# Attention scores of two heads at once: plain rows in halves of the array, rotary rows in quarters

## The reference

```python
def mla_dense(qn, qr, kn, kr, v):
    s = jnp.einsum('bqhd,bkhd->bhqk', qn, kn) + jnp.einsum('bqhd,bkd->bhqk', qr, kr)
    p = jax.nn.softmax(s.astype(jnp.float32) * MLA_SCALE, axis=-1).astype(v.dtype)
    return jnp.einsum('bhqk,bkhd->bqhd', p, v)
```

## Time and profile before

| | before |
|---|---|
| median of three runs | 4079.25 us (4078.5 to 4080.53) |
| profiled execution, its own time | 4078.63 us |
| its span | 4076.9 us |
| TensorE busy | 3979.0 us, 98% of the span |
| VectorE busy | 2047.5 us, 50% |
| ScalarE busy | 1070.0 us, 26% |
| L965, scores, TensorE, x800 records | 339.9 us |
| L1036 x2624 and L1026 x1280 | L1036 3% and L1026 2% of the chain that ended last |
| mean granted TensorE clock | 0.992 of full |

### The profile page before, as it was taken

How to read it: one execution, slowest core, us unless ns; L and a number is a source line. 1 busy time by engine, 2 the same in 40 slices (tenths; PEclk the granted TensorE clock), 3 DMA queues, 4 the chain that set the end, 5 groups by cost and what they waited for, 6 DMA issues and landing times.

```text
span 4076.9 us, 77681 instructions
## 1 busy us (share of the span) xinstructions
PE 3979.0 (98%) x31395; PEld 2863.8 (70%) x31396; DVE 2047.5 (50%) x4419; ACT 1070.0 (26%) x2422; POOL 305.1 (7%) x320
## 2 busy tenths in 40 slices
PE   8999999999999899999999999999999999999998
PEld 5565777655544688888888565777544448899997
DVE  1235676666645533333334444666544456444445
ACT  2335555400012111111111334555301121101013
POOL 0000000000000111111111000000000003010101
PEclk9999999999999899999999999999999999999999
DMA  6211000334434488888887221000333348999998
GB/s 212 67 54 62 19 19 19 104 103 118 121 112 156 161 265 273 268 265 266 266 266 229 88 72 62 19 19 19 94 109 88 117 174 255 325 329 326 330 326 281
DMA packets 559541, 658.02 MB, mean 161 GB/s; under 512 B 21284, under 2 KB 496120, under 8 KB 559352
## 3 DMA queue, kind: packets, MB, share of 16 engines
q1 hardware_dynamic: 527768, 564.10, 42.9%
q0 software_dynamic: 31008, 89.20, 7.7%
q10 hardware_dynamic: 576, 2.10, 0.1%
HBM read 582.92 MB, written 72.42 MB: 161 GB/s over the span
## 4 chain that ended last, share of the span: by engine, by line
PE 90%; DVE 4%; DVEq 2%; SPq 1%; DMA 1%; issue 1%; ACT 1%; POOL 0%; POOLq 0%; ACTq 0%
PE PS L750 37%; PE PS L1385 11%; PE PS L1416 9%; PE PS L754 8%; PE PS L965 7%; PE PS L1156 5%; PE PS L1036 3%; PE PS L870 2%; PE PS L1026 2%; DVE arena L1853 2%; SPq L493 1%; PE PS L1410 1%; PE PS L928 1%; DVE arena L2120 1%; DVEq L2124 1%
## 5 line engine op out<-in xcount | busy, mean ns | idle before, releaser
L750 PE MATMUL PS<-arena 128*128 128x160 f32 (+4 forms) x7004 | 1686.9, 402 | 10.9 <-DVE arena L1853 4.9
L750 PEld LDWEIGHTS PS<-arena 128*128 128x128 f32 x7004 | 1102.5, 190 | 567.9 <-issue 543.8
L1853 DVE TENSOR_TENSOR arena<-arena,PS 128x256 f32<-128x256 f32 (+3 forms) x661 | 290.6, 448 | 1035.0 <-ACT arena L1816 556.5
L1853 DVE TENSOR_TENSOR arena<-arena 128x1024 f32<-128x1024 f32 (+9 forms) x778 | 547.6, 721 | 129.2 <-PE PS L750 45.8
L754 PEld LDWEIGHTS PS<-arena 128*128 128x128 f32 (+1 forms) x2980 | 348.1, 142 | 197.4 <-issue 160.1
L754 PE MATMUL PS<-arena 128*128 128x128 f32 (+1 forms) x2980 | 436.7, 278 | 24.2 <-DMA arena<-x_mid,arena 15.4
L1385 PE MATMUL PS<-arena 128*64 128x128 f32 x8192 | 454.9, 273 | 1.6 <-DVE arena L1853 1.6
L1385 PEld LDWEIGHTS PS<-arena 128*64 128x64 f32 x8192 | 451.2, 137 | 5.2 <-DVE arena L1853 1.7
L1416 PE MATMUL PS<-arena 128*64 128x256 f32 x3600 | 396.0, 380 | 1.0 <-DVE arena L1853 0.5
L1816 ACT ACTIVATE arena<-PS 128x160 f32<-128x160 f32 (+1 forms) x256 | 74.5, 291 | 1177.2 <-PE PS L750 636.6
L1416 PEld LDWEIGHTS PS<-arena 128*64 128x64 f32 x3600 | 274.6, 137 | 117.0 <-issue 10.1
(11 more groups left out here) (274 smaller groups left out, 2635.9 us busy)
## 6 DMA issues: line engine op xcount, KB each, us to landing
arena<-in_w_exp_gate SPq DMA_DIRECT2D x128, 1024.0 KB, 7.3
arena<-in_w_exp_up SPq DMA_DIRECT2D x128, 1024.0 KB, 9.6
arena<-in_w_exp_down SPq DMA_DIRECT2D x128, 1024.0 KB, 7.6
arena<-in_w_ada POOLq DMA_DIRECT2D x40, 1024.0 KB, 5.6
arena<-in_w_in SPq DMA_DIRECT2D x32, 512.0 KB, 5.4
h_transposed<-arena SPq DMA_DIRECT2D x20, 512.0 KB, 3.9
q_latent_attn<-arena SPq DMA_DIRECT2D x18, 512.0 KB, 2.8
arena<-q_latent_attn SPq DMA_DIRECT2D x18, 512.0 KB, 3.5
```

The source lines that it names most:

```text
L750: m = pe.matmul(o, lt, rh, start=start and i == 0, stop=stop and i == n - 1)
L1853: return dve.tensor_tensor(o, x, y, op)
```

## The change

The scores of both heads of a unit are made together. Keys lie in two buffers: `kN`, plain rows, head A of a pair on partitions 0 to 63 and B on 64 to 127, and `kR`, the rotary key four times, on each quarter of the partitions. The queries of a tile likewise: four pairs of plain rows, four pairs of rotary rows with each head's twice (`qrx` is copied twice over). Per full unit the score products are: four of 32 rows and 512 keys, one in each quarter of the array (both heads, both key chunks), which start the accumulation; then two of 64 rows and 512 keys (one head in each half) for chunk 0, the same for chunk 1; and for the last 256 keys two of 32 rows and two of 64. A's scores are always in banks 0 to 2, B's in 3 to 5, the band in 0 to 2, the outputs in bank 5, the turned divisors in bank 7, and transposes take banks 6 and 7 in turn.

TensorE's order per unit becomes: long rotary products of the next unit, A's first transposes, plain products 0, A's second, plain products 1, A's third, W's first two, the last 256 keys of the next unit, W's third, B's three, band of the next unit, outputs of the window, outputs of A and B, divisors. ScalarE makes exp A and exp B of the next unit one after the other, with a new wait of each for the transposes that read the same buffer; VectorE copies A0, B0 and B1 (three chunks) and takes the maxima of both heads chunk by chunk. `band` is the former window part of `scores` with its set fixed and its wait changed to `pM` 2N+1. The projection writes keys, queries and rotary queries with one instruction each.

```diff
-qrx = at(R + 21248, MH + 1, 2 * ROPE)
+qrx = at(R + 21248, MH, 2, ROPE)
...
-kT = at(O, MH, TOK)
+kN = at(O, MH // 2, TOK)
+kR = at(O + 5120, TOK)
...
-def score_set(part, n):
-    return (3 * n + PART[part]) % 2 * 3
-def out_bank(n):
-    return score_set("A", n + 1) + 1
-def turned(part, n, ci, blocks):
-    b = 6 + ci % 2 if part == "W" else 7 - ci % 2
-    if part == "B" and ci == 2:
-        b = score_set("A", n + 1) + 2
-    return PS[:, b, 0:blocks * P]
...
-ON_DVE = {"A": (0,), "W": (0, 2), "B": (0,)}
+SET = {"A": 0, "W": 0, "B": 3}
+OUT = 5
+def turned(part, lp, ci, blocks):
+    nth = "AWB".index(part) * (3 if lp is not None else 1) + ci
+    return PS[:, 6 + nth % 2, 0:blocks * P]
+ON_DVE = {"A": (0,), "W": (), "B": (0, 1)}
...
-        def scores(p, lp, n, part):
...
+        def keys(p, lp, n):
...
+            def cols(i):
+                return slice(i * 512, min((i + 1) * 512, TOK if full else CTX))
+            def rotary(g, i, quad):
+                rows, k = slice(quad * ROPE, (quad + 1) * ROPE), cols(i)
+                pe.matmul(PS[:, 3 * g + i, 0:k.stop - k.start], qMt[rows, u, 4 + c, :], kR[rows, k], start=True, stop=False)
+            def plain(i):
+                k = cols(i)
+                for g in range(2):
+                    pe.matmul(PS[:, 3 * g + i, 0:k.stop - k.start], qMt[half(g), u, c, :], kN[half(g), c, k], start=False, stop=True).then_inc(s["sM"], 1)
+            def free():
+                if c == 0:
+                    pe.wait_ge(*s(f"q_in{u}", (p + n // 8) * 32 + 32))
+                if later(N):
+                    pe.wait_ge(*s("mxW", 2 * N))
+                    pe.wait_ge(*s("pM", 2 * N))
+            def short(i):
+                if not full:
                     free()
...
-            def some(i):
-                if i == order[0] and part == "A":
-                    if c == 0:
-                        pe.wait_ge(*s(f"q_in{u}", (p + n // 8) * 32 + 32))
-                    if later(N):
-                        pe.wait_ge(*s("mxW", 2 * N))
-                if i == order[0] and part == "B":
-                    pe.wait_ge(*s("pM", 2 * N + 1))
-                if i == 1 and part == "B" and later(N):
-                    pe.wait_ge(*s("ob", N))
-                cn = min(512, nk - i * 512)
-                pe.matmul(PS[:, b + i, 0:cn], qMt[0:rows, u, at_h, :], kT[0:rows, at_h, i * 512:i * 512 + cn], start=True, stop=True).then_inc(s["sM"], 1)
-            return [lambda i=i: some(i) for i in order]
-        def transposes(p, lp, n, part, ahead=False):
+                elif N > 1:
+                    pe.wait_ge(*s("ob", N - 1))
+                for g in range(2):
+                    rotary(g, i, 2 * g)
+                plain(i)
+            def long_rotary():
...
+                    for i in range(2):
+                        rotary(g, i, 2 * g + i)
+            return [long_rotary, lambda: plain(0), lambda: plain(1), lambda: short(2)] if full else [lambda: short(0)]
...
+                if later(N) and (part, ci) == (("A", 1) if full else ("W", 0)):
+                    pe.wait_ge(*s("rt_o", N))
...
-                elif (part, ci) == ("W", 2):
+                elif part == "W":
+                    pe.wait_ge(*s("pt_a", pa_count(l, lp, n, 1 + ci)))
+                elif part == "B" and ci < 2:
+                    pe.wait_ge(*s("pt_a", pa_count(l, lp, n, 4 + ci)))
+                elif part == "B":
                     pe.wait_ge(*s("pt_d", pd_count(l, lp, n, 2)))
-                elif (part, ci) == ("B", 0):
-                    pe.wait_ge(*s("pt_a", pa_count(l, lp, n, 3)))
-                elif (part, ci) == ("B", 1):
-                    pe.wait_ge(*s("pt_d", pd_count(l, lp, n, 3)))
-                elif (part, ci) == ("B", 2) and ahead:
...
-        def outputs(p, lp, n, ahead):
...
+        def band_outputs(p, lp, n, ahead):
...
-                if ahead:
-                    pe.wait_ge(*s("pM", 2 * N + 3))
+            if ahead:
+                pe.wait_ge(*s("pM", 2 * N + 4))
+            if later(N):
+                pe.wait_ge(*s("ob", N))
...
+            if not full:
                 pe.wait_ge(*s("pt_a", pa_count(l, lp, n, 3)))
             nm = 10 if full else 2
             for kt in range(nm):
-                if kt in (4, 8):
-                    pe.wait_ge(*s("pt_a", pa_count(l, lp, n, 3 + kt // 4)))
+                if kt == 4:
+                    pe.wait_ge(*s("pt_d", pd_count(l, lp, n, 3)))
+                if kt == 8:
+                    pe.wait_ge(*s("pt_a", pa_count(l, lp, n, 6)))
                 for g in range(2):
-                    pe.matmul(PS[half(g), o, P:2 * P], V[:, kt, half(2 * c + g)], PT[:, place("AB"[g], n, kt), :], start=kt == 0, stop=kt == nm - 1)
+                    pe.matmul(PS[half(g), OUT, P:2 * P], V[:, kt, half(2 * c + g)], PT[:, place("AB"[g], n, kt), :], start=kt == 0, stop=kt == nm - 1)
             pe.wait_ge(*s("rc", N + 1))
             for j in range(2):
-                m = tr(PS[:, o, (2 + j) * P:(3 + j) * P], rcb[:, j, :])
+                m = tr(PS[:, 7, j * P:(j + 1) * P], rcb[:, j, :])
             m.then_inc(s["pv"], 1)
...
-            for part in "AW":
-                weave(scores(p, lp, 0, part), [])
-            weave(scores(p, lp, 0, "B"), transposes(p, lp, 0, "A"))
+            weave(keys(p, lp, 0), [])
+            band(p, lp, 0)
         def pair(p, t0, lp, lp_next):
             for n in range(8):
                 nx = after(lp, n, lp_next)
-                keys = scores(p, *nx, "A") if nx else []
-                turns = transposes(p, lp, n, "W")
-                band = scores(p, *nx, "W") if nx else []
-                weave(keys[:2], turns[:1])
-                for step in keys[2:] + turns[1:] + band + transposes(p, lp, n, "B", bool(nx)):
+                ks = keys(p, *nx) if nx else []
+                turns = [step for part in "AWB" for step in transposes(p, lp, n, part)]
+                weave(ks[:3], turns[:3])
+                if lp is not None:
+                    order = turns[3:5] + ks[3:] + turns[5:]
+                else:
+                    order = ks[3:]
+                for step in order:
                     step()
-                outputs(p, lp, n, bool(nx))
                 if nx:
-                    weave(scores(p, *nx, "B"), transposes(p, *nx, "A"))
+                    band(p, *nx)
+                band_outputs(p, lp, n, bool(nx))
+                outputs(p, lp, n)
...
-                m = A(kT[half(g), g::2, ds(t * P, P)], heads(half(g), 5), ACT.Copy)
-            m.then_inc(s["kn"], 1)
+            A(kN[:, :, ds(t * P, P)], pairs(5), ACT.Copy).then_inc(s["kn"], 1)
...
-                    m = A(qMs[half(g), g::2, :], heads(half(g), 4), ACT.Copy, scale=MSCALE)
-                m.then_inc(s["qn"], 1)
+                A(qMs[:, 0:4, :], pairs(4), ACT.Copy, scale=MSCALE).then_inc(s["qn"], 1)
...
-            A(kT[NOPE:MQ, 0::2, ds(t * P, P)], PS[NOPE:MQ, 2, 0:P].unsqueeze(1).to_broadcast([ROPE, 4, P]), ACT.Copy)
-            A(kT[0:NOPE, 1::2, ds(t * P, P)], PS[0:NOPE, 2, 0:P].unsqueeze(1).to_broadcast([NOPE, 4, P]), ACT.Copy).then_inc(s["kT_cp"], 1)
+            A(kR[:, ds(t * P, P)], PS[:, 2, 0:P], ACT.Copy).then_inc(s["kT_cp"], 1)
...
+            if prev:
+                act.wait_ge(*s("tr", tr_count(l, *prev, part, len(chunks(part, *prev)) - 1)))
...
+                copy_chunks(p, lp, n, "A")
                 copy_chunks(p, lp, n, "W")
                 if nx:
-                    expo(p, *nx, "A")
+                    expo(p, *nx, "A", (lp, n))
+                    expo(p, *nx, "B", (lp, n))
                 copy_chunks(p, lp, n, "B")
                 if nx:
                     expo(p, *nx, "W")
                 rows_sum(p, n)
-                if nx:
-                    copy_chunks(p, *nx, "A")
-                    expo(p, *nx, "B")
...
-            rope(qrx[:, 1:, 0:ROPE], PS[:, 3, 0:MH * ROPE].rearrange("p (h c) -> p h c", h=MH), tab[:, 128:192], MH, 8, tmpm)
-            dve.drain()
-            dve.tensor_copy(qrx[:, 0, 0:ROPE], qrx[:, MH, 0:ROPE]).then_inc(s["qro"], 1)
+            rope(qrx[:, :, 0, :], PS[:, 3, 0:MH * ROPE].rearrange("p (h c) -> p h c", h=MH), tab[:, 128:192], MH, 8, tmpm)
+            dve.drain()
+            dve.tensor_copy(qrx[:, :, 1, :], qrx[:, :, 0, :]).then_inc(s["qro"], 1)
...
-            for g in range(2):
-                dve.tensor_scalar(qMs[half(g), 1 - g::2, :], PS[half(g), 3, :].rearrange("p (h c) -> p h c", h=4), MSCALE, None, ALU.mult).then_inc(s["qM_cp"], 1)
+            dve.tensor_scalar(qMs[:, 4:8, :].rearrange("p a b -> p (a b)"), PS[:, 3, :], MSCALE, None, ALU.mult).then_inc(s["qM_cp"], 2)
...
+                if nth == 0:
                     between()
-                dve.wait_ge(*s("sM", sM_count(l, lp, n, part, nth)))
-                dve.tensor_reduce(mxc[:, g, i:i + 1], PS[:, b + i, 0:min(512, TOK - i * 512)], AX.X, ALU.max)
-            dve.drain()
```

(73 more changed lines are left out.)

111 lines of the change are left out of this document (23 added, 88 removed).

## The result

The changed kernel takes 4232.41 us (median; 4230.65 to 4236.47) where the kernel before takes 4079.89 (4078.5 to 4081.17): a ratio of 1.0375, interval 1.0362 to 1.0388, 152.5 us slower. The forecast was 4244, with a range of 4185 to 4305. The profiled execution has a span of 4231.2 us, 154.3 more than before.

The account below looks back on a forecast made before the run. TensorE's own list bounds the kernel. Ordinary units +110, edge units +41, last units -8, context +13, first units +11 make 167; projection -2 gives +165 us, so 4244 us, range 4185 to 4305.

Parts of the forecast that it names:

- What bounds it: Attention's full units: bound by the length of TensorE's own list, which repeats after 12.81 us.
- Four quarters at once, -0.86: Score products per unit: rotary rows run in four array quarters at once, 3.44 us in place of 4.30.
- Rival (b): Rotary score passes: quarters run two at a time (4299 us) or one by one (4437); 14%.
- Eight more changes, +1.45: TensorE's order per unit: 12 changes of array division where there were 4, 5x0.20 + 3x0.15 = 1.45 us.
- Waits, +1.69: TensorE per unit: W1 waits 0.33 us for A2's copy; 1.36 us standing still behind B0's copy and exp B.
- Edge and last units: 16 band-edge units take 14.77 us, +41 us together; each layer's last unit takes 9.4, giving -8 us.
- Context and first units: Context units +0.9 us each, +13 with the turn to full ones; first unit of each layer +4 and +7.
- Projection: Before attention: fewer ScalarE and VectorE operations, VectorE's scaling then ending last; -1.1 us a layer, -2 in all.
- (a): Full units: divisions cost as said but the wait chain is covered, unit 13.40 us, 4141 in all; 5%, half-way cases 7%.
- (c): TensorE's clock falls during the 1.4 us of waits, passes doubling in parts: 64 x 3 us, 4436; 3%.
- (d): Full units: the saving of 0.86x64 = 55 us shows whole, 4024 us; 3%.
- (e): Whole kernel: saving and costs cancel, no difference, 4079 us; 1%.

Follow-up runs that it names:

- The control: Kernel before plus four small 16-column products on all 128 rows in every full unit, woven into transposes: 4123.29 us, against 4077.78.
- the order alone: Changed kernel with its order, banks, copies and waits, but scores from before's keys, queries and full-array products: 4191.15 us, ratio 1.0276.
- the kernel with products on 64 rows: Kernel before plus four small 16-column products on rows 0 to 63 in every full unit, woven into transposes: 4203.35 us, against 4077.78.
- products on 32 rows: Kernel before plus four small 16-column products on rows 0 to 31 in every full unit, woven into transposes: 4202.19 us, against 4077.78.

## Why the prediction was right, point by point

- **What bounds it.** TensorE's own list, 12.81 us a unit. The control bears this out: four small products of 0.17 us each by their starts lengthened the period by 0.71 (13.52).
- **Four quarters at once, -0.86.** Right. A quarter pass of 512 columns takes 1.07 us with its changes, a pass of halves 1.06, so four run as freely as two. Of the Trainium skill's 3.07x for four row tiles (TensorE: Matmul & The Clock Gate, Part 3), which would have added an estimated 0.39 us per unit, nothing is seen here: the two rotary passes side by side take 1.49 for 1.29 of columns, and the missing 0.20 is there with halves too. Rival (b) falls.
- **Eight more changes, +1.45.** Right in sum, within what the trace can tell: 14.88 - 12.81 + 0.86 less the waits of 1.47 leaves 1.46. From quarters to halves took 0.20 (0.63 from 628.72 to 629.35 for 0.43 of columns), where 0 to 0.4 was open. The Trainium skill's rule that a new tiling mode drains TensorE (TensorEngine Tiling (Array Packing), Key Properties) agrees; its price here is 0.15 to 0.2 us.
- **Waits, +1.69.** Right in kind, 0.2 too large. W1's was 0.26 (forecast 0.33). From W2's start to the outputs it is 3.96 us (629.98 to 633.95) where the sum had 4.11 (4.26 less the change ahead of it), so TensorE stands for 1.21 in place of 1.36. The term that was too large is the 0.16 from the end of a copy or an exponential to TensorE. It was read from the lengths of two records (0.70 against 0.60), but by starts it is 0.06: B0's copy ends at 631.94 (631.26 and 0.68) and B2 starts at 632.00, exp B ends at 633.89 and the outputs start at 633.95. The first maximum, on the other hand, starts 0.05 later than the sum has it (630.12, 0.14 behind W2's start, for 0.09), and the reductions take the 1.14 that were said. These 0.07 and 0.15 are the whole of 15.10 less 14.88, and of the 13 us by which the 62 periods fell short.
- **Edge and last units.** 14.56 for 14.77 and 9.08 for 9.4, by the same terms.
- **Context and first units.** A context unit takes 5.6 us (+0.9, as said). The first period is 7.79 instead, and the clock accounts for it: see below. +4.4 to the first copy was forecast at +3; the clock, lower there for longer than before, is the likely reason, and no run separates it.
- **Projection.** TensorE starts at 336.99 instead of 337.96, 0.97 earlier (forecast 1.1), and behind VectorE's scaling, which now ends last, as forecast:

```profile
335.98 0.69 DVE L1992 TENSOR_SCALAR arena<-PS 128x512 f32<-128x512 f32 x1 [3.93 <-PE PS L742]
...
336.99 0.70 PE L904 MATMUL PS<-arena 32*128 32x256 f32 x4 [1.15 <-DVE arena L1992]
```

- **The other rivals.** (a), the chain covered: no, the waits are in every unit. (c), the clock halved inside units: no, 1.00 from 480 to 870 us; only its small form holds, at the start and at the turn to full units (0.83 from 395 to 405 us). (d) and (e): no gain shows, since the order alone loses 113 us before the tiling is made.

The rest of the program, +2.1 us, isn't explained; the same stretch differs by up to 5 us among the kernels here (1156.5 to 1162.0) which are alike in it. Not tried: the outputs in the columns of bank 5 that B's last 256 keys leave free (256 to 511). Exp B doesn't read them, so the outputs might not have to wait for it.

## What to carry over

Price a change of the array's division at 0.15 to 0.2 us each and count the changes before the columns saved: eight of them ate 0.86 us of saved streaming and 0.6 more. Then ask what the moved work covered: most of the loss here (113 of 153 us) came with the new order, which puts two heads' scores next to each other and leaves a chain of reductions, a copy and an exponential with too little TensorE work beside it. A new order is judged by walking that chain with durations from the trace; it gave the unit within 0.22 of 14.88 us.

## What was not expected of the hardware

The granted clock falls at two places where TensorE stands still for a while beside little work. The first is the first context unit. Sums over the same stretches, before and after:

```profile
345.00:352.00 7.00, 6.79 (x52) 0.82 0.00 1
352.00:360.00 8.00, 7.17 (x58) 1.00 0.13 36
```

```profile
345.00:352.00 7.00, 6.29 (x34) 0.50 0.00 1
352.00:360.00 8.00, 7.06 (x44) 0.69 0.01 2
```

In the kernel before the clock is at the lower level (1.2 GHz) here too, but for less long: 0.50 from 343 to 347 us, 1.00 from 349 on. After the change it is 0.50 from 340 to 352 and 1.00 only from 360 on. Before, TensorE had waited 1.92 us for an exponential (341.21); after, 2.82 and 1.60 us for an exponential and the masked scores' maximum (341.14 and 343.96). The first context period takes 7.79 us for 5.6. An estimate from the row of 0.69 agrees: 5.0 of its 8 us are at the lower level, which is 2.5 us of work at full clock lost.

The second is in the kernel with products on 64 rows, where a layer's last unit took 15.85 us (11.53 in the control). Its sums over stretches, and those of the control at the same place:

```profile
840.00:845.00 5.00, 3.67 (x17) 0.78 1.22 278
845.00:850.00 5.00, 5.00 (x48) 0.54 1.15 301
```

```profile
800.00:805.00 5.00, 3.99 (x22) 1.00 1.21 274
805.00:810.00 5.00, 4.60 (x70) 1.00 1.22 273
```

The one lost the clock, the other, with TensorE idle at the same place, kept it. With products on 64 rows it happened in both layers, with products on 32 rows in one of the two (15.85 and 12.71 us). It cost 3.1 us each time and is no part of what a change of division costs; what decides it isn't settled here.

A wait costs TensorE a little more than its length: of the transposes behind it, the second starts 0.165 us after the first instead of 0.109. The same 0.165 stands behind every change of division, wait or not (the divisors' two transposes at 637.37 and 637.54). The first product behind a change starts 0.20 us after the last one ahead of it in place of 0.11; these two pieces, 0.09 and 0.06, are the 0.15 of a change back to the full array.
